# A hybrid attention/Mamba-2/PEER block: one quarter of the experts computed densely beside the gathers

## What is computed

```python
    top_s, pos = lax.top_k(cand_s, PEER_TOPK)
    eid = jnp.take_along_axis(cand_i, pos, axis=-1)
    gate = jax.nn.softmax(top_s, axis=-1).astype(h.dtype)
...
        u = peer_u[eb]
        act = jax.nn.gelu(jnp.einsum('bthkd,btd->bthk', u, hb), approximate=False)
        vv = peer_v[eb]
        return jnp.einsum('bthk,bthkd->btd', gb * act, vv)
```

## Time and profile before

| | |
|---|---|
| three runs | 2724.50, 2725.55 (median), 2726.16 us |
| the profiled execution | 2721.7 us, its span 2720.0 us |
| mean granted clock of PE | 0.818 |
| busy share of the span | PE 64%, DVE 61%, ACT 29%, POOL 26% |
| bytes moved by DMA | 765.8 MB, 541.1 MB of them from POOL's queue |

### The profile page before, as it was taken

One profiled execution on the slowest core, in us unless ns is written; L12 is line 12 of the kernel. 1 busy time (PEld: TensorE's weight loads), 2 busy tenths in 40 slices (PEclk: granted clock), 3 DMA queues, 4 the chain that ended last, 5 costly groups with the idle time before them and its releaser, 6 DMA issues.

```text
span 2720.0 us, 30150 instructions
## 1 busy us (share of the span) xinstructions
PE 1741.3 (64%) x10135; PEld 1314.5 (48%) x10135; DVE 1663.1 (61%) x2765; ACT 798.1 (29%) x1313; POOL 715.9 (26%) x620
## 2 busy tenths in 40 slices
PE   7899999999999999999980223223222233232234
PEld 6799888988988888878880000000000000000001
DVE  5888646556556556575689666656666656665530
ACT  4456445545545545544423000000000000000000
POOL 1000011001000000040025654455444345444332
PEclk9799999999999999999985666666566566666677
DMA  5244554554554554557587999999999999999998
GB/s 180 81 155 136 173 181 152 162 173 149 165 171 150 163 173 149 159 161 241 176 325 276 412 420 420 420 420 420 420 419 419 418 418 416 419 417 420 420 387 325
DMA packets 209756, 765.81 MB, mean 282 GB/s; under 512 B 18776, under 2 KB 53904, under 8 KB 143248
## 3 DMA queue, kind: packets, MB, share of 16 engines
q0 software_dynamic: 74432, 541.10, 48.3%
q1 hardware_dynamic: 134832, 223.61, 26.0%
q10 hardware_dynamic: 416, 0.16, 0.0%
HBM read 762.70 MB, written 2.10 MB: 281 GB/s over the span
## 4 chain that ended last, share of the span: by engine, by line
PE 45%; DMA 29%; DVE 14%; issue 6%; POOL 4%; ACT 1%; DVEq 0%; POOLq 0%; ACTq 0%; SPq 0%
DMA u_slots<-in_peer_u_dram,eid 25%; DVE u_slots L1354 6%; PE accA L1482 5%; PE accA L1483 5%; PE accA L1484 5%; PE accB L1482 4%; PE accB L1483 4%; PE accB L1484 4%; DMA v_slots<-in_peer_v_dram,v_eid 3%; PE accB L1474 2%; PE accB L1476 2%; PE accB L1475 2%; POOL v_slots L624 2%; DVE weight L1370 2%; POOL u_slots L614 2%
## 5 line engine op out<-in xcount | busy, mean ns | idle before, releaser
L1354 DVE CUSTOM_DVE_ANT_0 u_slots<-u_slots,h 128x2048 f32<-128x2048 f32 x256 | 583.8, 2291 | 429.7 <-DMA u_slots<-in_peer_u_dram,eid 426.8
L962 DVE TENSOR_TENSOR w_lo<-w_raw,w_hi 128x1024 fp32r<-128x1024 f32 (+1 forms) x420 | 522.5, 1254 | 355.0 <-ACT w_hi L657 353.5
L657 ACT ACTIVATE w_hi<-w_raw 128x1024 fp32r<-128x1024 f32 (+1 forms) x420 | 441.4, 1057 | 418.6 <-PE accB L1484 141.2
L614 POOL DMA_INDIRECT u_slots<-in_peer_u_dram,eid x256 | 310.7, 1214 | 726.4 <-DVE dots L1354 512.0
L1817 PE MATMUL accA<-v_slots,weight 128*32 128x512 f32 x512 | 113.9, 1039 | 527.5 <-DMA v_slots<-in_peer_v_dram,v_eid 527.5
L1817 PE MATMUL small<-v_slots,weight 128*32 128x512 f32 x512 | 112.6, 1027 | 388.9 <-DMA v_slots<-in_peer_v_dram,v_eid 388.9
L624 POOL DMA_INDIRECT v_slots<-in_peer_v_dram,v_eid x256 | 300.5, 1174 | 130.3 <-issue 77.3
L1817 PEld LDWEIGHTS accA<-v_slots,weight 128*32 128x32 f32 x512 | 21.7, 158 | 596.1 <-issue 596.1
L1817 PEld LDWEIGHTS small<-v_slots,weight 128*32 128x32 f32 x512 | 21.6, 156 | 457.7 <-issue 457.7
L905 ACT ACTIVATE gate<-pair_v,g_max 128x16 f32<-128x16 f32 x16 | 4.9, 308 | 535.1 <-DVE g_max L1327 535.0
L583 POOL TENSOR_TENSOR y_skip<-x_tok,per_head_g 128x512 f32<-128x512 f32 x16 | 24.2, 1534 | 473.5 <-ACT x_tok L864 473.5
(11 more groups left out here) (370 smaller groups left out, 3988.0 us busy)
## 6 DMA issues: line engine op xcount, KB each, us to landing
w_raw<-in_w_in_dram SPq DMA_DIRECT2D x168, 512.0 KB, 3.5
w_raw<-in_w_in_dram SPq DMA_DIRECT2D x128, 256.0 KB, 3.0
w_raw<-in_w_o_ssm_dram SPq DMA_DIRECT2D x64, 512.0 KB, 4.0
w_raw<-in_w_o_attn_dram SPq DMA_DIRECT2D x32, 512.0 KB, 4.6
w_raw<-in_w_out_dram SPq DMA_DIRECT2D x32, 512.0 KB, 4.4
w_raw<-in_w_peer_q_dram SPq DMA_DIRECT2D x32, 512.0 KB, 4.7
w_raw<-in_w_uq_dram SPq DMA_DIRECT2D x8, 512.0 KB, 6.1
w_raw<-in_w_ukv_dram SPq DMA_DIRECT2D x8, 512.0 KB, 4.2
```

What stands on the lines that cost most here:

```text
L614: pool.indirect_dma_start(u_slots[:, n % U_RING, :], None, peer_u[0], bass.IndirectOffsetOnAxis(ap=eid[:, u, k:k + 1], axis=0)).then_inc(u ...
L657: act.activation(w_hi[:, slot, :, 0:w], w_raw[:, slot, :, 0:w], ACT.Copy).then_inc(hi_split, 1)
L962: dve.tensor_tensor(w_lo[:, slot, :, 0:w], w_raw[:, slot, :, 0:w], w_hi[:, slot, :, 0:w].bitcast(F32), ALU.subtract).then_inc(lo_split, 1)
L1354: dve.tensor_tensor_reduce(slot, slot, h2[:, u // PH, :], 1.0, 0.0, ALU.mult, ALU.add, dots[:, u, k:k + 1]).then_inc(u_free, 1)
```

## The change

The experts of blocks 96 to 127 are no longer gathered. `gather_u` and `gather_v` get a bound, `bounds_check=LAST_GATHERED`, so that rows above it are skipped (the first use of each slot still takes all rows). What these experts contribute is computed for all 256 tokens:

- **Dense U.** SP loads the 32 blocks of `peer_u` whole (1 MB each, two buffers `ud`). PE transposes a block in 4 quarters (`turn_quarter`, 4 transposes of 128x128), ACT copies each from PSUM (`take_quarter`), PE multiplies it with the transposed `h2_t` (4 matmuls of 256 columns into `pair_d`, `dense_quarters`), and ACT takes the gelu of a finished block (`take_block`). 28 of the 128 quarters come before everything else, then 5 before each group of V, in units 0 to 4 of PE's loop.
- **Gates.** In PE's units 5 and 6 the gates of the skipped experts are brought into the dense form in 16 lots of 16 tokens: ACT makes the one-hot of the second key (`second_keys`: 16 squares of 128 columns, then one relu of 2048), DVE the one-hot of the first key times the gate (`first_keys`), PE multiplies them (`scatter_gates`, 16 matmuls of 32 columns), and DVE multiplies the result into the dense gelus (`gate_lot`).
- **Dense V.** SP loads the 32 blocks of `peer_v` (four buffers `vd`). In PE's units 8 to 15 each V group is followed by 2 or 3 halves (`dense_halves`: one block for one tile, 4 matmuls of 512 columns), which sum in the same PSUM banks.

To have all gates by unit 5, `top_experts` is called for 3, 4, 4, 3 and 2 units in units 0 to 4 (`top_units`). ACT makes gelu(u), and only then exp and id spread of these units. `norm_gate` divides the gate and sets it to zero where the expert is dense. `x1` is pushed into PSUM by PE, so that `merge` goes and copies take its place. A dot writes to a small `junk` tile instead of its slot. `LEAD` is now counted in gathers: U is 20 ahead of V.

```diff
 
-        LEAD = 2
+
+        LEAD = PK + 4
+
+        FIRST_DENSE = NK - DENSE
+        LAST_GATHERED = FIRST_DENSE * NK - 1
+        QUARTERS = 4 * DENSE
+        EARLY_QUARTERS = 28
+        DENSE_UNITS = 5
+        LOTS = T // LOT
+
+        def top_units(u):
+
+            return (range(3), range(3, 7), range(7, 11), range(11, 14), range(14, 16))[u] if u < 5 else range(0)
+
+        def quarters_before(u, q):
+
+            n = QUARTERS - EARLY_QUARTERS
+            i = 4 * u + q
+            return n * (i + 1) // (4 * DENSE_UNITS) - n * i // (4 * DENSE_UNITS)
+
+        def halves_before(i):
+
+            return 2 * DENSE * min(i + 1, 29) // 29 - 2 * DENSE * min(i, 29) // 29
...
+            sp.wait_ge(w_used, n_all)
+            for b in range(DENSE):
+                if b >= 2:
+                    sp.wait_ge(ut_full, 4 * (b - 1))
+                sp.dma_start(ud[:, b % 2, :], peer_u[0, (FIRST_DENSE + b) * NK:(FIRST_DENSE + b + 1) * NK, :]
+                             ).then_inc(ud_landed[b % 2], 16)
...
+                    sp.wait_ge(x1_pushed, NT)
+                elif b >= 4:
+                    sp.wait_ge(vd_free, b - 3)
+                sp.dma_start(vd[b % 4][:, :], peer_v[0, (FIRST_DENSE + b) * NK:(FIRST_DENSE + b + 1) * NK, :]
+                             ).then_inc(vd_landed[b % 4], 16)
...
                 pool.indirect_dma_start(u_slots[:, n % U_RING, :], None, peer_u[0],
-                                        bass.IndirectOffsetOnAxis(ap=eid[:, u, k:k + 1], axis=0)
+                                        bass.IndirectOffsetOnAxis(ap=eid[:, u, k:k + 1], axis=0),
+                                        bounds_check=LAST_GATHERED if n >= U_RING else NK * NK - 1, oob_is_err=False
...
-            for u in range(LEAD):
-                pool.wait_ge(unit_ids, u + 1)
-                for k in range(PK):
-                    gather_u(u, k)
...
+            for n in range(LEAD):
...
-            for u in range(UNITS):
-                if u + LEAD < UNITS:
-                    pool.wait_ge(unit_ids, u + LEAD + 1)
-                pool.wait_ge(v_ids, u + 1)
-                for k in range(PK):
-                    if u + LEAD < UNITS:
-                        gather_u(u + LEAD, k)
-                    gather_v(u, k)
+            for n in range(PK * UNITS):
+                if n + LEAD < PK * UNITS:
+                    next_u(n + LEAD)
+                if n % PK == 0:
+                    pool.wait_ge(v_ids, n // PK + 1)
+                gather_v(n // PK, n % PK)
...
-            for u in range(UNITS):
-                if u + LEAD < UNITS:
-                    unit_softmax(u + LEAD)
-                    spread_ids(u + LEAD)
...
+            def take_quarters(n):
+                for i in range(taken[0], taken[0] + n):
+                    if i + 1 < QUARTERS:
+                        take_quarter(i + 1)
+                    if i % 4 == 3:
+                        take_block(i // 4)
+                taken[0] += n
+
+            def unit_gelu(u):
...
+                act.activation(gelu[:, u % 2, :], dots[:, u % 2, :], ACT.Gelu).then_inc(gelued, 1)
+                for v in top_units(u):
+                    if v >= 2:
+                        unit_softmax(v)
+                        spread_ids(v)
...
+            def second_keys(j):
+
+                if j >= 2:
+                    act.wait_ge(g_full, j - 1)
+                for i in range(LOT):
+                    ins = act.activation(one_second[j % 2][:, i, :], iota[:, :], ACT.Square,
+                                         bias=picks_t[:, 2, j * LOT + i:j * LOT + i + 1])
...
+                act.activation(one_second[j % 2][:, :, :], one_second[j % 2][:, :, :], ACT.Relu, scale=-1.0,
+                               bias=iota[:, 1:2]).then_inc(second_ready, 1)
+
+            take_quarter(0)
+            take_quarters(EARLY_QUARTERS)
+            unit_gelu(0)
+            for u in range(PH):
+                if u == DENSE_UNITS:
...
+                for q in range(4):
+                    if u < DENSE_UNITS:
+                        take_quarters(quarters_before(u, q))
+                    elif u < DENSE_UNITS + 2:
+                        for j in range(2):
+                            second_keys(8 * (u - DENSE_UNITS) + 2 * q + j)
+                    if q == 3:
+                        unit_gelu(u + 1)
+            for u in range(PH + 1, UNITS):
+                unit_gelu(u)
...
                     slot = u_slots[:, i % U_RING, :]
-                    dve.tensor_tensor_reduce(slot, slot, h2[:, u // PH, :], 1.0, 0.0, ALU.mult, ALU.add,
-                                             dots[:, u, k:k + 1]).then_inc(u_free, 1)
-
-            def weights_of(u):
+                    dve.tensor_tensor_reduce(junk[min(u, 1)][:, i % 2, :], slot,
+                                             h2[:, 0, :] if u < PH else h2_late[:, :], 1.0, 0.0, ALU.mult, ALU.add,
...
+            def norm_gate(u):
 
                 dve.wait_ge(gate_exp, u + 1)
                 step(dve.reciprocal(g_inv[:, 0:1], g_sum[:, u:u + 1]))
+                step(dve.tensor_scalar(gate[:, u, :], gate[:, u, :], g_inv[:, 0:1], None, ALU.mult))
+                dve.scalar_tensor_tensor(gm[:, u, :], first[:, u, :], float(FIRST_DENSE), gate[:, u, :], ALU.is_lt,
+                                         ALU.mult).then_inc(normed, 1)
+
+            def weights_of(u):
+
+                dve.wait_ge(normed, u + 1)
                 dve.wait_ge(gelued, u + 1)
-                dve.scalar_tensor_tensor(share[:, u, :], gelu[:, u, :], g_inv[:, 0:1], gate[:, u, :], ALU.mult,
-                                         ALU.mult).then_inc(shared, 1)
+                dve.tensor_tensor(share[:, u % 2, :], gelu[:, u % 2, :], gm[:, u, :], ALU.mult).then_inc(shared, 1)
...
+            def gate_lot(j):
+
+                dve.wait_ge(g_full, j + 1)
+                gates = small[:, j % 2, :].rearrange("p (t b) -> p b t", b=DENSE)
+                n = DENSE // 4
+                for i in range(4):
+                    o = dense[i][:, :, j * LOT:(j + 1) * LOT]
+                    ins = dve.tensor_tensor(o, o, gates[:, i * n:(i + 1) * n, :], ALU.mult)
+                ins.then_inc(g_taken, 1)
...
             for u in range(1, UNITS):
                 some_dots(u, 0, 4)
+                for v in top_units(u - 1):
+                    norm_gate(v)
                 weights_of(u - 1)
                 dotted = [4]
 
-                def four_dots():
-                    some_dots(u, dotted[0], 4)
-                    dotted[0] += 4
-
-                if u + LEAD < UNITS:
-                    top_experts(u + LEAD, four_dots)
-                else:
-                    four_dots()
-                    four_dots()
-                some_dots(u, 12, 4)
-                if u == PH + LEAD:
-                    merge(0)
+                def dots_to(n):
+                    some_dots(u, dotted[0], n - dotted[0])
+                    dotted[0] = n
+
+                calls = 2 * len(top_units(u))
+                called = [0]
+
+                def between():
+                    called[0] += 1
+                    dots_to(4 + 12 * called[0] // calls)
+
+                for v in top_units(u):
+                    top_experts(v, between)
+                if u == DENSE_UNITS + 1:
+                    dve.wait_ge(picks_turned, NT)
+                    first_keys(0)
+                    first_keys(1)
+                if 0 <= u - DENSE_UNITS - 1 < 2:
+                    for i in range(8):
+                        j = 8 * (u - DENSE_UNITS - 1) + i
+                        dots_to(4 + 12 * (i + 1) // 8)
+                        if j == 0:
+                            dve.wait_ge(d_taken, DENSE)
+                        gate_lot(j)
+                        if j + 2 < LOTS:
+                            first_keys(j + 2)
+                dots_to(PK)
             weights_of(UNITS - 1)
-            merge(1)
+            dve.wait_ge(v_free, 4 * UNITS)
+            for c in (1, 3):
+                dve.tensor_copy(u_slots[:, 0, c * BANK:(c + 1) * BANK], (small, pair_d)[c // 2][:, 1, :]
+                                ).then_inc(merged_dve, 1)
 
 
         @block.tensor
...
+            def dense_quarters(n):
+                for i in range(quartered[0], quartered[0] + n):
+                    b, q = i // 4, i % 4
+                    if i + 1 < QUARTERS:
+                        turn_quarter(i + 1)
+                    pe.wait_ge(ut_done, i + 1)
+                    if q == 0 and b >= 2:
+                        pe.wait_ge(d_taken, b - 1)
+                    for c in range(4):
+                        ins = pe.matmul(pair_d[:, b % 2, 0:T], ut[:, i % 2, c, :], h2_t[:, 4 * q + c, :],
+                                        start=q == 0 and c == 0, stop=q == 3 and c == 3)
+                    ins.then_inc(ut_used, 1)
+                quartered[0] += n
+
...
+            def scatter_gates(j):
+
...
+            def dense_halves(n):
```

(26 more changed lines are left out.)

250 lines of the change are left out of this document (214 added, 36 removed).

## The result

The changed kernel takes **2770.73 us** (median of 4 runs, 2767.69 to 2771.65), the kernel before 2725.03 in the same comparison: ratio **1.0165**, 95% interval 1.0148 to 1.0183. It is 1.7% slower, where 1.0% faster was forecast (2698 us). The stated range (2615 to 2790) held the time, the sign was wrong. The profiled execution has a span of 2769.9 us, 49.9 more than before.

The account below looks back on a forecast made before the run. DMA bytes were taken to bound the gather stage. 2129 us up to W(8), 470 for gathers, 70 for V loads and 28 for the end sum to 2697; the forecast was 2698 us, range 2615 to 2790.

Parts of the forecast that it names:

- The stage is bound by bytes; 2.50 us a full gather: Gather stage: 16 DMA engines always busy at 419 GB/s, 2.50 us for each gather of 128 rows of 8 KB.
- W(8): W(u) is the time DVE comes to the weights of unit u; for unit 8 the forecast was 2129 us.
- Uneven rows, s = 0.07: Gathers with skipped rows: unevenly filled DMA engines add a loss s of 0.07, making a unit of 32 gathers 64 us.
- a DMA share of 0.90 to 0.95: Sign from unit 8 on: DMA share below 1.01, as engines run dry unevenly.
- The start, W(0) 1519: Unit 0: 28 quarters ahead of ACT's gelu make DVE wait from 1452 us; its weights are done at 1519.
- Units 1 to 4 are DVE's: Early units: dots, fourteen `top_experts` and waits for exps set the pace, then DMA from the step to 1852 us at unit 4.
- Units 5 to 7, 200 us: Unit 5 takes 64 us, units 6 and 7 with the lots 68 each; bounds 60 and 80 for these two.
- V slots held by PE: Rival, units 8 to 15: POOL's queue stops at V gathers whose slots PE holds; 2811 us, half effect 2760; chance 0.13.
- Even rows: Rival: s = 0 and units 6 and 7 at 62 us; end at 2641 us, or 2625; chance 0.17.
- full price: Rival: fixed engines with s of 0.12 to 0.14, a unit of 67 to 68 us, end at 2741; chance 0.13.
- PE's clock: Rival: PE at 1.2 GHz, a quarter 4.3 us, units 1 to 5 PE's at 106 us, end at 2900; chance 0.05.
- Rows are not saved: Rival, gathers: a skipped row still costs its place, so the end comes at 2890 us; chance 0.05.

Follow-up runs that it names:

- all_rows: The changed kernel with the bound opened on every gather, so all rows are fetched while all dense work stays: 2945.64 us, one run.
- no_scatter: The changed kernel without the sixteen lots, so the dense gelus are not weighted by the gates: 2712.52 us, one run.
- early4: The changed kernel with 4 instead of 28 quarters ahead of the gelu of unit 0: 2715.43 us, ratio to before 0.9963.
- early4_lag: early4 with each lot's product with the gates taken four dots later on DVE: 2667.54 us, ratio to before 0.9791.
- early4_lag_lead24: early4_lag with U 24 gathers ahead of V instead of 20: 2814.98 us, ratio 1.0323.
- early4_lead16: early4 with U 16 gathers ahead of V instead of 20, and no lag: 2657.85 us, ratio 0.9753.
- bound_alone: The kernel before with only the bound on its gathers after the rings' first, the skipped experts' part missing from the output: 2551.15 us, one run.

## Why the prediction was wrong, point by point

- **The stage is bound by bytes; 2.50 us a full gather.** Right for the kernel before and for the last eight units: all_rows took 679.1 us from W(8), where (235 + 28) x 2.50 + 28 = 685.5. Wrong as a picture of units 0 to 7, where the share of DMA was 0.88 and 0.79.
- **Uneven rows, s = 0.07.** Right in size, and partly by luck: from W(8) on an even share would give 235 x 1.87 + 70 + 28 = 537, measured 569.7, so s = 33/439 = 0.075; no_scatter's units of 65 say the same. But the reason was engines that run dry, for which I named a DMA share of 0.90 to 0.95, and it was 0.99 at 399 GB/s, where full rows had 1.01 at 418. Of this loss of 4.5% only 2% is in the share. The 8 KB packets took 321 ns on average (315 before), another 2%. The 11146 packets of 4 bytes between 2200 and 2704 us, 9 ns each, are 6 of 504 us; some 7200 of them stand for skipped rows, the others, 16 for each gather or load, are there before too. Why a packet takes longer, and which engine moves which row, no run here tells.
- **The start, W(0) 1519.** Right (1515.3), and so was its mechanism: DVE waited 61.6 us for ACT's exp behind the quarters' copies. early4 shows that it was avoidable.
- **Units 1 to 4 are DVE's.** Right in time within 8 us up to W(2) (1704.4 against 1697), 26 us short at W(4) (1878.4 against 1852). DVE was busy 320 of 431 us. It waited for ACT's exps 10.1, 10.4, 8.5 and 11.9 us in the steps from W(0) to W(4), where I took 10, 10, 6 and 2.5: right at first, undersized later. The copies in front of the exps are held by PE's V groups, as the lead shows (22.9 to 30.1 us a step with 24 gathers, none with 16), and I costed ACT's own work only. And I took the longer of DVE and DMA for the step to W(4), 76.5 us; in 88.8 both waits stand one behind the other, 11.9 for exps and 14.4 for rows.
- **Units 5 to 7, 200 us: this step failed.** Its sentence was "All three engines hand over in turn, so I take 68 rather than 64". The prices of the work were right: ACT 4.79 + 2.00 us a lot (6.8 forecast), DVE 0.88 + 0.68 + 0.69 = 2.25 (2.3 forecast). PE's own part was not costed (4.5 us a lot). The hand-overs, for which I added 4 us a unit and at most 16, were what was mis-sized: even the upper bound, 80 us for a unit with lots, was under the 99 and 89 measured (the third unit took 66). Without lots the three units take 195 us (no_scatter), with them 254. What I missed is that two in-order queues beside the three engines close a ring. The last gather of V's third group in unit 5 stands in POOL's queue behind a U gather that needs 108 dots; ahead of the 108th DVE takes the product of lot 4; and PE makes lot 4 right in front of that same group. So its rows can only be called for when the lot is done, and landing is paid in full: PE waited 9.9 us there, 14.6 before the fourth group. Four dots of lag on DVE, with all work kept, took 43 us out of the stretch (early4_lag), and a lead that takes the slack away again brought 34 back (early4_lag_lead24). The row was there to be read: both the lead of 20 and the place of each lot are in the change.
- **The rivals.** The measured time lies where "V slots held by PE" put it (2760 to 2811), but not for its reason: in units 8 to 14 POOL waited 28.9 us of 504 for PE, and those units took what the forecast said. "Even rows" and "full price" fall with s = 0.075. Rows were saved (404.96 MB gathered instead of 541.1), PE's clock was 0.86 in units 0 to 4 and a quarter took 2.17 us (2.15 forecast). "Rows are not saved" has a slip in its sum: 1519 + 484 x 2.50 + 137 is 2866, and 2894 with the 28 us of the end, not 2890. A rival of the right mechanism was missing.

Against the kernel before, the change saved 74 us behind W(8) and lost 124 ahead of it. By the runs, 55 of these are the early quarters and 44 the order of dots and lots. Without both the idea is worth 2.1% to 2.5%, as early4_lag (2667.5) and early4_lead16 (2657.9) show; the bytes alone promised 6% (165 us).

## What to carry to other kernels

When a change ties a third engine into a pipeline whose engines all work in order, write down for one step who stands behind whom in **every** queue, the DMA issue queue included, and count the slack between them in steps: if a closed path has none, its whole latency is paid each round (24.5 us here), however little work there is. In this profile the ring shows itself as engines that are all 44 to 61% busy, DMA at 79%, each waiting for the next. Then shift one member by a few steps before making anything faster, and look at the other side, since slack given here is taken there.

## What was not expected of the hardware

- **A gather issued by POOL while DVE runs a dot is held to the dot's end.** Alone it takes 0.94 us (0.99 with a bound), held up to 3.1 us. In the kernel before it is the same (all 51 gathers issued under a dot between 1740 and 2580 us end 0.81 us behind it), but hidden (POOL still waited 120.4 of 300 us for dots, 1750 to 2050 us of the kernel before); with a quarter of the rows gone and nothing else changed it set the pace: 68.8 us a unit, 64.8 with dots of half the length.
- **Skipped rows keep their place in the queue, but cost next to nothing.** The packets of POOL's queue are as many as before, the bytes 404.96 MB instead of 541.1 (before, then after):

```profile
q0 software_dynamic: 74432, 541.10, 48.3%
...
q0 software_dynamic: 74432, 404.96, 37.4%
```
- **DMA busy and yet slower.** With rows left out a share of 0.99 stood for 399 GB/s, where 1.01 had been 418. The share shows less than half of that loss; the bytes per second show all of it. In bound_alone (1600 to 2400 us) the 8 KB packets took 338 ns at a share of 0.95 and 364 GB/s.
